# Convolution taps on 32x32 array tiles, four at once, in place of full 128x128 diagonals

## The chip, the cores and the metric

The kernel runs on one core of one Trainium2 chip, in float32 throughout. The metric is device microseconds of one launch; lower is better. Engines are named by what they do: TensorE multiplies matrices (PE in the profile, PEld for its weight loads), VectorE (DVE), ScalarE (ACT) and GpSimd (POOL) do elementwise work, SyncE (SP) issues DMAs.

## The reference

One inference step of a two-layer decoder for 256 prompt rows and 8 sample rows. Each layer is an FFN, a mixer, an FFN. The mixer projects to all its parts at once, and one of them is a depthwise convolution with 31 taps over 256 channels:

```python
def conv_mixer(a, prev, dw, dw_bias, ln_g, ln_b, pw):
    g = a[..., :CONV_W] * jax.nn.sigmoid(a[..., CONV_W:])
    buf = jnp.concatenate([prev.astype(g.dtype), g], axis=1)
    y = lax.conv_general_dilated(buf, dw[:, None, :].astype(g.dtype), window_strides=(1,),
                                 padding='VALID', dimension_numbers=('NWC', 'WIO', 'NWC'),
                                 feature_group_count=CONV_W) + dw_bias
    y = jax.nn.silu(layernorm(y, ln_g, ln_b)) @ pw
    return y, buf[:, -(CONV_K - 1):]
```

Beside it the mixer has a pooling part, sparse attention of the prompt (top 64 of up to 256 keys, chosen by an indexer) and sparse attention of the samples (top 256 of 1025 keys in paged caches of keys and values, 8 pages a sample).

## The kernel before

Channels lie on the 128 partitions and the 264 rows along the free dimension. All weights come as units of 128x1024 (512 KB), 318 in all. SyncE loads a unit into `raw`, ScalarE rounds it into `w_hi` (L338), VectorE makes the remainder `w_lo` (L555), and TensorE multiplies in three passes (L984 to L986), 24 matmuls a unit. Buffers are few (six raw, three split), so each engine is held to the pace of the others. Every engine has its program written out by hand, in order, with semaphore waits; nothing is rescheduled.

In the mixer, TensorE runs 15 projection units. VectorE takes each out of PSUM (`plain`, L642), applies the rotary embedding (`perm` on TensorE, then `rope`), and finds the samples' top 256 by a radix search of eight digits: VectorE counts (`count`, L713), TensorE sums the counts (`digit`, L1078), VectorE reads the digit (L720) and counts again. So TensorE and VectorE hand the search to and fro, one digit a unit, while the projection goes on.

The convolution of the prompt stands between these. For tap k and channel half c, ScalarE makes a 128x128 diagonal of the tap's weights (`taps`, L413, from the identity), into a ring of four pairs, and TensorE multiplies it with the gated input `gp`, shifted by k columns (L1091), and accumulates all 31 taps in PSUM bank 7. The taps are drawn in eleven pieces: 3 after unit 8, 3 after unit 9, 2 behind each of units 10 to 13, 3 after unit 14, 5 beside the keys, 5 and 4 before and after the eighth digit. ScalarE then adds the bias (L462).

After the last tap TensorE computes the prompt's scores (L1200), VectorE masks them (`masked`, L851), ScalarE exponentiates, VectorE divides (`norm`, L862), TensorE transposes (L1231) and multiplies with the values (L1241), and VectorE makes the low part of a head's output (`heads_out`, L886). The samples' keys are multiplied in `keys(b)` (L1188): 0 to 3 before the scores, and 4 to 7 one in each of the four head steps, ahead of that step's output. SyncE fetches the keys and values of samples 4 to 7 (L243): after the weight load that waits for the fourteenth split of the mixer it reads 48 page numbers from the table, loads the first values (L256), then the keys, 32 loads of 64 KB. GpSimd, after unit 14, stores the indexer keys (L1390), fetches 16 value pages (L1394) and stores the pooling state (L1398, L1399, 2048 runs of 60 bytes), then computes the pooling sums.

Of the kernel before, what the change touches and what calls it, by code (L numbers as in the profile page):

```python
# [14 lines left out]
AL = mybir.AluOpType  # L15
# [27 lines left out]
DW = 56  # L43
# [20 lines left out]

PAIRS = 4

# [15 lines left out]
    tanh=2, glu=2, tap=CK, conv=CK, conv_p=1, c_sum=1, c_cent=1, c_sq=1, c_var=1, c_rms=1, c_norm=1, c_silu=1,  # L82
# [9 lines left out]
def build(nc, xT, wts, par, cst, ptab, digits, kT, vC, kxT, scT, spT,  # L92
          yT, okT, ovT, okiT, ocP, ocS, opP, opS):
    ctx = ExitStack()
    with ctx:
# [40 lines left out]
        s_kx = [at[0]]  # L136
        kx = place("kx", [128, 4, PAST], F32)
        kx_end = at[0]
        kv = place("kv", [128, KV, PAST], F32)
# [24 lines left out]
        diag = place("diag", [128, 2 * PAIRS, 128], F32, [s2[0]])  # L164
# [20 lines left out]
        pTs = place("pTs", [128, NPG, 64], F32, s_kx)  # L185
        dg = place("dg", [64, 64], F32)
# [31 lines left out]
        ones = con[:, C_ONE:C_ONE + 128]  # L218

# [113 lines left out]
        def _(act):  # L333
# [67 lines left out]
            def mixer(L):  # L401
                u0 = U_MIX

                taken = [0]

                def taps(upto):

                    for k in range(taken[0], upto):
                        if k >= PAIRS:
                            act.wait_ge(sem["conv"], at_layer(L, "conv", k - PAIRS + 1))  # L410
                        for c in range(2):
                            w = DW + CK * c + k
                            ins = act.activation(diag[:, 2 * (k % PAIRS) + c, :], ident, ACT.Copy,  # L413
                                                 scale=pars[:, w:w + 1])
                        ins.then_inc(sem["tap"], 1)
                    taken[0] = upto

# [24 lines left out]
                taps(4)  # L442
# [5 lines left out]
                taps(8)  # L448
# [9 lines left out]
                taps(CK)  # L458

                act.wait_ge(sem["conv"], at_layer(L, "conv", CK))  # L460
# [86 lines left out]
        def _(dve):  # L547
# [86 lines left out]
            def mixer(L):  # L634
# [92 lines left out]
                dve.wait_ge(tables, 64)  # L727
                dve.wait_ge(sem["rstd"], at_layer(L, "rstd", 1))
# [57 lines left out]
                rope(ak[:, :], 3)  # L786
# [13 lines left out]
                rope(aq[:, 1, :], 3)  # L800
# [10 lines left out]
                for c in range(2):  # L811
# [3 lines left out]
                    if c == 0:  # L815
                        rope(aq[:, 3, :], 3)
# [55 lines left out]
                def equals():  # L872

                    dve.wait_ge(sem["conv"], at_layer(L, "conv", CK))
# [106 lines left out]
        def _(pe):  # L981
# [79 lines left out]
            def mixer(L):  # L1061
# [19 lines left out]
                drawn = [0]  # L1081

                def taps(upto):

                    for k in range(drawn[0], upto):
                        if k == 0:
                            pe.wait_ge(sem["glu"], at_layer(L, "glu", 2))
                            pe.wait_ge(sem["idx_relu"], at_layer(L, "idx_relu", 4))
                        pe.wait_ge(sem["tap"], at_layer(L, "tap", k + 1))
                        for c in range(2):  # L1090
                            ins = pe.matmul(PS[:, 7, NP * c:NP * c + NP], diag[:, 2 * (k % PAIRS) + c, :],  # L1091
                                            gp[:, c, k:k + NP], start=(k == 0 and c == 0), stop=(k == CK - 1),
                                            skip_group_check=True)
                        ins.then_inc(sem["conv"], 1)
                    drawn[0] = upto
# [50 lines left out]
                perm(7, ak[:, :], 3).then_inc(sem["perm"], 1)  # L1146
                taps(3)
                unit(9)

                pe.wait_ge(sem["chunk"], at_layer(L, "chunk", 9))  # L1150
# [4 lines left out]
                taps(6)  # L1155
                pe.wait_ge(sem["v_nat"], at_layer(L, "v_nat", 1))
                digit(0)
                unit(10)
                perm(9, aq[:, 0, :], 2).then_inc(sem["perm"], 1)
                taps(8)  # L1160
                digit(1)
                unit(11)
                pe.wait_ge(sem["rope"], at_layer(L, "rope", 4))
                perm(10, aq[:, 1, :], 3).then_inc(sem["perm"], 1)
                taps(10)
                digit(2)
                unit(12)
                pe.wait_ge(sem["rope"], at_layer(L, "rope", 5))
                perm(11, aq[:, 2, :], 2).then_inc(sem["perm"], 1)
                taps(12)  # L1170
                digit(3)
                unit(13)
                pe.wait_ge(sem["rope"], at_layer(L, "rope", 6))
                perm(12, aq[:, 3, :], 3).then_inc(sem["perm"], 1)
                taps(14)
                digit(4)
                unit(14)
                taps(17)
# [27 lines left out]
                for b in range(KV):  # L1206
                    keys(b)
                    if b == 1:
                        taps(22)
                        digit(6)  # L1210
                taps(27)
                digit(7)
                taps(CK)
# [130 lines left out]
        def _(pool):  # L1344
# [26 lines left out]
            with pool.Fori(0, DEPTH) as L:  # L1371
# [16 lines left out]
                pool.wait_ge(tables, 64)  # L1388
# [157 lines left out]
```

## Time and profile before

| | |
|---|---|
| runs (median; lowest to highest) | 1262.84 us; 1260.96 to 1262.85 us |
| profiled execution | 1260.21 us, span 1258.7 us, mean granted TensorE clock 0.964 |
| TensorE busy | 1162.6 us (92%), 8680 matmul records |
| VectorE busy | 794.2 us (63%) |
| ScalarE busy | 577.0 us (46%) |
| GpSimd busy | 196.0 us (16%) |
| HBM | 153 GB/s over the span |

A float32 matmul leaves two records in the profile, one for each of its passes; the rounded passes L984 to L986 leave one. The granted clock of TensorE is a share of 2.4 GHz and stands at 1.0 or at 0.5. A busy TensorE means only that a record is open, since records of one stream overlap.

### The profile page before, as it was taken

What the parts mean: (1) busy time and instruction counts of PE and PEld (TensorE: products, weight loads), DVE (VectorE), ACT (ScalarE), POOL (GpSimd) and SP (SyncE); (2) the same over time, 40 slices, a digit from 0 to 9 for tenths busy, and PEclk for the clock granted to TensorE, in tenths of its full rate; (3) what the DMA queues carried; (4) which work ended last, traced back from release to release, by engine and by line L of the source; (5) the groups of instructions that cost most, each with busy time, mean ns of one, the idle gap of its engine ahead of it and who ended that gap; (6) DMA issues with size and microseconds to landing.
All of it is one profiled execution on the core that took longest, in us unless ns stands there. A gap on an engine that the chain in (4) does not pass through costs nothing.

```text
span 1258.7 us, 27509 instructions
## 1 busy us (share of the span) xinstructions
PE 1162.6 (92%) x8680; PEld 1085.4 (86%) x8680; DVE 794.2 (63%) x1261; ACT 577.0 (46%) x976; POOL 196.0 (16%) x213
## 2 busy tenths in 40 slices
PE   4999999899779799999889999989996789999996
PEld 4999999778559799999889999977973689999994
DVE  3666644878744766664566665467877357666546
ACT  4444434444344544443454444353544445444435
POOL 0212100201500312110131211020024012121002
PEclk9999999899889899999989999989998899999998
DMA  7455565341643255555436555644418243555551
GB/s 239 164 214 189 178 220 201 111 127 62 116 133 117 69 193 176 183 183 182 135 89 213 183 182 189 226 153 136 101 57 136 85 133 127 184 174 185 182 166 37
DMA packets 91928, 192.92 MB, mean 153 GB/s; under 512 B 11986, under 2 KB 50066, under 8 KB 91730
## 3 DMA queue, kind: packets, MB, share of 16 engines
q1 hardware_dynamic: 89874, 187.58, 45.8%
q0 software_dynamic: 1984, 4.47, 1.6%
q8 instruction: 36, 0.59, 0.2%
q14 instruction: 34, 0.28, 0.1%
HBM read 189.42 MB, written 2.59 MB: 153 GB/s over the span
## 4 chain that ended last, share of the span: by engine, by line
PE 53%; issue 38%; POOL 3%; POOLq 2%; ACT 2%; DVE 1%; DMA 1%; DVEq 0%; SPq 0%; ACTq 0%
PE PS L984 16%; PE PS L985 15%; PE PS L986 15%; PE PS L1010 2%; PE PS L1091 2%; PE PS L1134 1%; POOLq L1393 1%; POOL h L1368 1%; DMA raw<-in_wts 1%; PE PS L1073 1%; ACT w_hi L338 1%; POOL vx L1394 1%; POOLq L1394 0%; DVE w_lo L555 0%; POOL pw L1409 0%
## 5 line engine op out<-in xcount | busy, mean ns | idle before, releaser
L555 DVE TENSOR_TENSOR w_lo<-raw,w_hi 128x1024 fp32r<-128x1024 f32 x312 | 409.4, 1312 | 324.1 <-ACT w_hi L338 321.9
L984 PE MATMUL PS<-x_hi,w_hi 128*128 128x264 f32 x1648 | 487.5, 296 | 10.3 <-DVE w_lo L555 10.3
L985 PE MATMUL PS<-x_lo,w_hi 128*128 128x264 f32 x1648 | 471.9, 286 | 0.0
L986 PE MATMUL PS<-x_hi,w_lo 128*128 128x264 f32 x1648 | 471.6, 286 | 0.0
L338 ACT ACTIVATE w_hi<-raw 128x1024 fp32r<-128x1024 f32 x312 | 328.0, 1054 | 238.0 <-PE PS L986 236.9
L984 PEld LDWEIGHTS PS<-x_hi,w_hi 128*128 128x128 f32 x1648 | 315.6, 192 | 14.5 <-DVE w_lo L555 11.2
L985 PEld LDWEIGHTS PS<-x_lo,w_hi 128*128 128x128 f32 x1648 | 315.8, 192 | 2.5
L986 PEld LDWEIGHTS PS<-x_hi,w_lo 128*128 128x128 f32 x1648 | 313.9, 190 | 0.0
L984 PE MATMUL PS<-h_hi,w_hi 128*128 (+1 forms) x832 | 237.5, 285 | 3.1 <-issue 3.1
L986 PE MATMUL PS<-h_hi,w_lo 128*128 (+1 forms) x832 | 237.1, 285 | 0.0
L985 PE MATMUL PS<-h_lo,w_hi 128*128 (+1 forms) x832 | 236.5, 284 | 0.0
L1357 POOL TENSOR_TENSOR us<-gs,us 128x264 f32<-128x264 f32 x88 | 97.0, 1103 | 437.6 <-DVE us L604 437.6
L984 PEld LDWEIGHTS PS<-h_hi,w_hi 128*128 128x128 f32 x832 | 156.6, 188 | 3.9 <-issue 3.9
L985 PEld LDWEIGHTS PS<-h_lo,w_hi 128*128 128x128 f32 x832 | 157.2, 189 | 0.0
L986 PEld LDWEIGHTS PS<-h_hi,w_lo 128*128 128x128 f32 x832 | 156.9, 189 | 0.0
L377 ACT ACTIVATE gs<-gs 128x264 f32<-128x264 f32 x88 | 37.3, 424 | 198.8 <-DVE gs L598 198.8
L1368 POOL TENSOR_TENSOR h<-h,y 128x264 f32<-128x264 f32 x48 | 44.2, 930 | 434.1 <-DVE y L584 434.1
L1010 PE MATMUL PS<-sq,con 128*128 128x264 f32 x96 | 36.7, 469 | 39.2 <-ACT sq L350 24.0
L1091 PE MATMUL PS<-gp,diag 128*128 128x256 f32 x248 | 57.9, 382 | 0.4 <-ACT diag L413 0.4
L1091 PEld LDWEIGHTS PS<-gp,diag 128*128 128x128 f32 x248 | 46.1, 189 | 10.5 <-ACT diag L413 2.8
L598 DVE TENSOR_TENSOR gs<-PS,rstd 128x264 f32<-128x264 f32 x88 | 38.0, 432 | 25.5 <-PE PS L986 20.1
L1010 PEld LDWEIGHTS PS<-sq,con 128*128 128x128 f32 x96 | 18.3, 233 | 41.2 <-ACT sq L350 26.1
(244 smaller groups left out, 977.2 us busy)
## 6 DMA issues: line engine op xcount, KB each, us to landing
raw<-in_wts SPq DMA_DIRECT2D x315, 512.0 KB, 3.8
kv<-in_kT SPq DMA_DIRECT2D x128, 64.0 KB, 2.5
kx<-in_kxT SPq DMA_DIRECT2D x128, 32.0 KB, 2.1
kv<-in_vC SPq DMA_DIRECT2D x64, 64.0 KB, 1.9
vx<-in_vC POOLq DMA_DIRECT2D x32, 64.0 KB, 2.1
vx<-in_vC SPq DMA_DIRECT2D x32, 64.0 KB, 2.0
h<-in_xT SPq DMA_DIRECT2D x1, 1056.0 KB, 4.9
out_yT<-h SPq DMA_DIRECT2D x8, 132.0 KB, 1.7
```

Source lines behind the costliest of these rows:

```text
L338: act.activation(w_hi[:, u % SPLIT, :], raw[:, u % RAW, :], ACT.Copy).then_inc(sem["w_hi"], 1)
L377: act.activation(gs[:, f % 3, :], gs[:, f % 3, :], ACT.Silu).then_inc(sem["silu"], 1)
L555: tt(w_lo[:, u % SPLIT, :], raw[:, u % RAW, :], w_hi[:, u % SPLIT, :].bitcast(F32), AL.subtract).then_inc(sem["w_lo"], 1)
L598: tt(gs[:, f % 3, :], PS[:, 2 * (f % 3), 0:NT], rstd[:, :], AL.mult).then_inc(sem["gs"], 1)
L984: pe.matmul(out, w_hi[:, w, cols], hi, start=start, stop=False)
L985: pe.matmul(out, w_hi[:, w, cols], lo, start=False, stop=False)
L986: return pe.matmul(out, w_lo[:, w, cols], hi, start=False, stop=stop)
L1010: pe.matmul(PS[:, 7, 0:NT], ones, sq[:, d, :], start=(d == 0), stop=(d == KD - 1)).then_inc(sem["mm_pre"], 1)
L1073: return pe.matmul(PS[:, bank, 0:NT], con[:, which:which + 128], x, start=True, stop=True)
L1091: ins = pe.matmul(PS[:, 7, NP * c:NP * c + NP], diag[:, 2 * (k % PAIRS) + c, :], gp[:, c, k:k + NP], start=(k == 0 and c == 0), stop=(k == ...
L1357: pool.tensor_tensor(us[:, f % 3, :], gs[:, f % 3, :], us[:, f % 3, :], AL.mult).then_inc(sem["mid"], 1)
L1368: pool.tensor_tensor(h[:, d, :], h[:, d, :], y[:, d, :], AL.add).then_inc(sem["h_new"], 1)
```

## The change

The channels are cut into groups of 32, four in each half. A tap of one group is a 32x32 diagonal. It is multiplied on one of the 16 array tiles: the row tile is the channel group i, the column tile j is that of the tap, k = 4r + j. So a round r covers four taps at once. A row tile i accumulates in its own PSUM bank (3, 4, 5, 7), and column tile j writes partitions 32j to 32j + 31 of it, so that after eight rounds each bank holds four partial sums, one over the other. The calls of `taps` are now four, of two rounds each, after units 9 to 12.

ScalarE copies the four banks to `cpart`, and `fold` multiplies them with `stack`, an identity of 32 columns stacked four times, which adds the four partial sums and puts each channel group in its place in bank 7. GpSimd makes all tap tiles `dgw` at once, in two instructions of 128x992, from `stack` and the weights. `dgw` and `cpart` lie where the indexer's cached keys `kx` lay, so GpSimd waits until these are read. VectorE makes `stack` from the identity ahead of the first chunk. The perms use bank 2 alone, and wait for the rope before.

```diff
-                def taps(upto):
-
-                    for k in range(taken[0], upto):
-                        if k >= PAIRS:
-                            act.wait_ge(sem["conv"], at_layer(L, "conv", k - PAIRS + 1))
-                        for c in range(2):
-                            w = DW + CK * c + k
-                            ins = act.activation(diag[:, 2 * (k % PAIRS) + c, :], ident, ACT.Copy,
-                                                 scale=pars[:, w:w + 1])
-                        ins.then_inc(sem["tap"], 1)
...
-                for m, upto in ((12, 10), (13, 12), (14, 14), (15, 17), (16, 17), (17, 19)):
+                for m in range(12, 18):
                     split(L, u0 + m)
-                    taps(upto)
+                    if m == 15:
+                        act.wait_ge(sem["conv"], at_layer(L, "conv", 1))
+                        for i, bank in enumerate(CONV_BANKS):
+                            act.activation(cpart[:, i, :], PS[:, bank, :], ACT.Copy).then_inc(sem["c_part"], 1)
...
-                taps(CK)
-
-                act.wait_ge(sem["conv"], at_layer(L, "conv", CK))
+
+                act.wait_ge(sem["c_fold"], at_layer(L, "c_fold", 1))
...
                 dve.wait_ge(tables, 64)
+                dve.tensor_reduce(stack[:, :], ident.rearrange("p (q c) -> p c q", q=4), AX.X, AL.add) \
+                    .then_inc(sem["stack"], 1)
                 dve.wait_ge(sem["rstd"], at_layer(L, "rstd", 1))
...
                 def equals():
-
-                    dve.wait_ge(sem["conv"], at_layer(L, "conv", CK))
...
+                def taps(first, rounds):
+
+                    for r in range(first, first + rounds):
                         for c in range(2):
...
+                            for j in range(4):
+                                k = 4 * r + j
+                                for i, bank in enumerate(CONV_BANKS):
+                                    if k < CK:
+                                        rows = slice(32 * i, 32 * i + 32)
+                                        ins = pe.matmul(PS[32 * j:32 * j + 32, bank, NP * c:NP * c + NP],
+                                                        dgw[rows, c, k, :], gp[rows, c, k:k + NP],
+                                                        start=(r == 0 and c == 0), stop=(k + 4 >= CK),
+                                                        skip_group_check=True)
...
+                def fold():
+
+                    pe.wait_ge(sem["c_part"], at_layer(L, "c_part", 4))
+                    for i in range(4):
+                        ins = pe.matmul(PS[32 * i:32 * i + 32, 7, :], stack[:, :], cpart[:, i, :],
+                                        start=True, stop=True)
+                    ins.then_inc(sem["c_fold"], 1)
...
+                pe.wait_ge(sem["glu"], at_layer(L, "glu", 2))
+                pe.wait_ge(sem["diag"], at_layer(L, "diag", 2))
+                pe.wait_ge(sem["idx_relu"], at_layer(L, "idx_relu", 4))
...
+                pool.wait_ge(tables, 64)
+                pool.wait_ge(sem["stack"], at_layer(L, "stack", 1))
+                pool.wait_ge(sem["idx_d"], at_layer(L, "idx_d", 1))
+                for c in range(2):
+                    pool.tensor_tensor(dgw[:, c, :, :],
+                                       stack[:, :].unsqueeze(1).to_broadcast([128, CK, 32]),
+                                       pars[:, DW + CK * c:DW + CK * c + CK].unsqueeze(2).to_broadcast([128, CK, 32]),
+                                       AL.mult).then_inc(sem["diag"], 1)
```

TensorE, before, between unit 10 and unit 11 (L1073 is a perm, L1091 a tap of both halves, L1078 a digit):

```order
849 L1073 MATMUL PS<-aq,con 128x264 [waits chunk]
850 L1089 REGISTER_ALU
851 L1091 MATMUL PS<-gp,diag 128x256 [waits tap]
852 L1091 MATMUL PS<-gp,diag 128x256
853 L1089 REGISTER_ALU
854 L1091 MATMUL PS<-gp,diag 128x256 [waits tap]
855 L1091 MATMUL PS<-gp,diag 128x256
856 L1078 MATMUL PS<-rad,con 128x1 [waits count]
```

The same place after the change (L1061 is the perm, L1078 the taps, L1066 the digit):

```order
833 L1061 MATMUL PS<-aq,con 128x264 [waits chunk]
834 L1078 MATMUL PS<-gp,dgw 32x256 x64
835 L1066 MATMUL PS<-rad,con 128x1 [waits count]
836 L977 REGISTER_ALU
```

Four matmuls of the full array have become 64 of one tile each.

TensorE, before, from the seventh digit to the first scores (L1188 are the keys of samples 2 and 3, L1200 and L1201 the scores):

```order
1018 L1078 MATMUL PS<-rad,con 128x1 [waits count]
1019 L1188 MATMUL PS<-kv,LA 64x512 [waits kv_full2]
1020 L1188 MATMUL PS<-kv,LA 64x512
1021 L1188 MATMUL PS<-kv,LA 64x512 [waits kv_full3]
1022 L1188 MATMUL PS<-kv,LA 64x512
1023 L1089 REGISTER_ALU
1024 L1091 MATMUL PS<-gp,diag 128x256 [waits tap]
```

The same stretch after, up to the scores:

```order
958 L1066 MATMUL PS<-rad,con 128x1 [waits count]
959 L1187 MATMUL PS<-kv,LA 64x512 [waits kv_full2]
960 L1187 MATMUL PS<-kv,LA 64x512
961 L1187 MATMUL PS<-kv,LA 64x512 [waits kv_full3]
962 L1187 MATMUL PS<-kv,LA 64x512
963 L1065 REGISTER_ALU
964 L1066 MATMUL PS<-rad,con 128x1 [waits count]
965 L1199 MATMUL PS<-ak,aq 128x256 [waits rope]
```

No tap stands here any more: the eighth digit and the scores follow the keys directly.

## Rows read from the trace of the kernel before

**Rows 1.** Conv taps: group (count, busy us, mean ns), then timeline (start us, us).
```profile
L1091 PE MATMUL PS<-gp,diag 128*128 128x256 f32 x248 | 57.9, 382 | 0.4 <-ACT diag L413 0.4
...
271.54 2.75 PE L1091 MATMUL PS<-gp,diag 128*128 128x256 f32 x12
...
311.04 4.59 PE L1091 MATMUL PS<-gp,diag 128*128 128x256 f32 x20
```

**Rows 2.** Timeline of VectorE, layer 0; idle us before and its releaser in brackets.
```profile
272.57 1.23 DVE L555 TENSOR_TENSOR w_lo<-raw,w_hi 128x1024 fp32r<-128x1024 f32 x1 [2.58 <-ACT w_hi L338]
...
291.24 0.16 DVE L720 TENSOR_SCALAR radi<-PS 128x1 int32<-128x1 f32 x1 [0.45 <-PE PS L1078]
...
293.38 1.23 DVE L555 TENSOR_TENSOR w_lo<-raw,w_hi 128x1024 fp32r<-128x1024 f32 x1
...
301.85 0.16 DVE L720 TENSOR_SCALAR radi<-PS 128x1 int32<-128x1 f32 x1 [1.94 <-PE PS L1078]
...
328.44 0.96 DVE L851 TENSOR_TENSOR sp__106<-PS,bias 128x768 f32<-128x768 f32 x1 [6.61 <-PE PS L1201]
```

**Rows 3.** Timeline of TensorE where it uses part of the array.
```profile
251.03 1.68 PE L1125 MATMUL PS<-ki,qi 64*128 64x256 f32 x16
...
375.21 0.27 PE L1280 MATMUL PS<-kv,pTs 128*8 128x128 f32 x1
375.31 0.27 PE L1280 MATMUL PS<-vx,pTs 128*8 128x128 f32 x1
375.32 0.27 PE L1280 MATMUL PS<-kv,pTs 128*8 128x128 f32 x1
...
262.64 0.39 PE L1138 MATMUL PS<-kn,LQ 128*32 128x1 f32 x8
```

**Rows 4.** Prices of GpSimd and ScalarE: group, timeline, and ScalarE's PSUM copy (ns).
```profile
L1357 POOL TENSOR_TENSOR us<-gs,us 128x264 f32<-128x264 f32 x88 | 97.0, 1103 | 437.6 <-DVE us L604 437.6
...
338.24 2.30 POOL L1408 COPY pw<-pa 64x256 f32<-64x256 f32 x1
...
L440 ACT ACTIVATE X<-PS x1: 1027/1027/1027, 268.2 to 268.2; 128x1024 f32<-128x1024 f32 x1
```

**Rows 5.** Timeline of SyncE's and GpSimd's DMA issues and TensorE, layer 0.
```profile
305.48 0.55 POOL L1390 DMA_DIRECT2D out_okiT<-ki  x1 [27.27 <-PE PS L986]
...
331.48 1.28 POOL L1399 DMA_DIRECT2D out_opS<-stp  x1
...
321.99 5.08 SPq L256 DMA_DIRECT2D vx<-in_vC  x8
327.25 17.16 SPq L243 DMA_DIRECT2D kv<-in_kT  x32
...
339.69 2.49 PE L1188 MATMUL PS<-kv,LA 128*64 128x512 f32 x4
```

**Rows 6.** Tile kv in 330.9 to 331.3, then in 332.5 to 335.5: issue to landing.
```profile
L243 SPq DMA_DIRECT2D kv<-in_kT x1: 345/345/345, 330.9 to 330.9; - x1
...
DMA to landing us min/median/max: 2.1/2.1/2.1
...
L243 SPq DMA_DIRECT2D kv<-in_kT x6: 345/346/346, 332.5 to 335.2; - x6
...
DMA to landing us min/median/max: 7.5/8.3/8.5
```

**Rows 7.** Windows (clock is 0.60), VectorE's first head output twice, layer 1's store and load.
```profile
328.40:339.70 11.30, 4.72 (x23) 3.56 (x23) 10.92 (x19) 4.70 (x18) 9.39 (x12) 0.60 0.93 110
...
347.11 0.42 DVE L886 TENSOR_TENSOR h_lo<-PS,h_hi 128x256 fp32r<-128x256 f32 x1
...
964.93 0.42 DVE L886 TENSOR_TENSOR h_lo<-PS,h_hi 128x256 fp32r<-128x256 f32 x1
...
947.98 1.28 POOL L1399 DMA_DIRECT2D out_opS<-stp  x1
...
L243 SPq DMA_DIRECT2D kv<-in_kT x1: 345/345/345, 948.7 to 948.7; - x1
```

More of the change, by code:

```diff
@@ L81 @@
     o_shi=1, o_slo=1, dg=1,
-    tanh=2, glu=2, tap=CK, conv=CK, conv_p=1, c_sum=1, c_cent=1, c_sq=1, c_var=1, c_rms=1, c_norm=1, c_silu=1,
+    tanh=2, glu=2, stack=1, diag=2, conv=1, c_part=4, c_fold=1, conv_p=1, c_sum=1, c_cent=1, c_sq=1, c_var=1, c_rms=1, c_norm=1, c_silu=1,
     c_hi=1, c_lo=1, c_out=1, c_ohi=1, c_olo=1,
@@ L185, in build @@
         pTs = place("pTs", [128, NPG, 64], F32, s_kx)
+        stack = place("stack", [128, 32], F32)
         dg = place("dg", [64, 64], F32)
@@ L218, in build @@
         ones = con[:, C_ONE:C_ONE + 128]
+        CONV_BANKS = (3, 4, 5, 7)
         def at_layer(L, name, k):
@@ L785, in mixer @@
                 counted_ = count_above_zero()
-                rope(ak[:, :], 3)
+                rope(ak[:, :], 2)
                 signs(counted_)
@@ L799, in mixer @@
                 plain(11, aq[:, 2, :])
-                rope(aq[:, 1, :], 3)
+                rope(aq[:, 1, :], 2)
                 digit(2)
@@ L815, in mixer @@
                     if c == 0:
-                        rope(aq[:, 3, :], 3)
+                        rope(aq[:, 3, :], 2)
                         dve.wait_ge(sem["rope"], at_layer(L, "rope", 8))
@@ L1079, in digit @@
                               start=True, stop=True).then_inc(sem["digit"], 1)
[L1081 to L1089, printed above, removed]
-                        for c in range(2):
-                            ins = pe.matmul(PS[:, 7, NP * c:NP * c + NP], diag[:, 2 * (k % PAIRS) + c, :],
-                                            gp[:, c, k:k + NP], start=(k == 0 and c == 0), stop=(k == CK - 1),
-                                            skip_group_check=True)
-                        ins.then_inc(sem["conv"], 1)
-                    drawn[0] = upto
+                def taps(first, rounds):
+                    for r in range(first, first + rounds):
+                        for c in range(2):
+                            for j in range(4):
[7 more added lines that the diff above has]
+                                                        skip_group_check=True)
+                    if first + rounds == 8:
+                        ins.then_inc(sem["conv"], 1)
+                def fold():
[4 more added lines that the diff above has]
+                    ins.then_inc(sem["c_fold"], 1)
                 first_units(L, 0, u0)
@@ L1145, in mixer @@
                 unit(8)
-                perm(7, ak[:, :], 3).then_inc(sem["perm"], 1)
-                taps(3)
+                perm(7, ak[:, :], 2).then_inc(sem["perm"], 1)
                 unit(9)
+                pe.wait_ge(sem["glu"], at_layer(L, "glu", 2))
+                pe.wait_ge(sem["diag"], at_layer(L, "diag", 2))
+                pe.wait_ge(sem["idx_relu"], at_layer(L, "idx_relu", 4))
                 pe.wait_ge(sem["chunk"], at_layer(L, "chunk", 9))
@@ L1154, in mixer @@
                 ins.then_inc(sem["v_t"], 1)
-                taps(6)
+                taps(0, 2)
                 pe.wait_ge(sem["v_nat"], at_layer(L, "v_nat", 1))
```

34 lines of the change are left out of this document (14 added, 20 removed).

## The prediction

> **What bounds the kernel now.** I read the page first, then TensorE's timeline through the conv taps, VectorE's beside it, and last the queues of SyncE and GpSimd. The page puts TensorE at 92% of the span; the taps are 248 records of 0.382 us [rows 1]. A run of twenty of them stands beside the keys at 311.04. A record is one pass: each float32 matmul leaves two, and 124 records a layer are 31 taps x 2 channel halves x 2 passes. In a run of twelve they start (2.75 - 0.38)/11 = 0.215 us apart [rows 1], so a layer spends 124 x 0.215 = 26.7 us on them. They stand in eleven pieces between projection units, digits of the top-k search and keys.
>
> VectorE's timeline shows who waits. Its idle stretches in layer 0 [rows 2] are 2.58 us for the high half of unit 10, which ScalarE made late because it drew tap diagonals first; 0.25 us, 0.45 and 0.45 before three digits (one stands there); 1.94 us before the fifth digit; 0.23 us at the seventh; and 6.61 us before the first masked scores, at 328.44. With 2.2 us of the first these make 12.1 us in which VectorE waited for TensorE or ScalarE only because the taps stood in line. After 328.44 VectorE is the one that is waited for. The second layer repeats this 617.0 us later.
>
> **What the 16 tiles cost.** The new code issues 248 matmuls of 256 columns a layer, so 496 records, 128 in each of three calls and 112 in the last. If all tiles stream side by side, one tile has 8 records in a call and a call takes 8 x 0.215 = 1.72 us, as much as two taps did; the layer has four calls, 6.9 us. Nothing in the trace runs 16 tiles, so I bound it. For tiles running side by side speak two places [rows 3]: sixteen records on two row tiles (eight each, 4 of 256 and 4 of 128 columns, one stream of which would be 4 x 0.215 + 4 x 0.109 = 1.3 us) take 1.68 us with the last one's latency, where one stream would be 2.6; and two column tiles (names vx and kv) each start a pass every 0.11 us, 0.01 us apart from each other. The second tile starts although the first still has passes queued, so the second pass of each matmul does not hold the next tile. The upper side: on one 32-column tile with one moving column, eight records take 0.39 us [rows 3], and their mean spacing without the last latency (0.17) is about 0.031 us; 128 x 0.031 = 4.0 us a call. The lower side is 1.72. I take 1.72 plus an estimated 0.25 for leaving and entering the full-array form (the two-row-tile block shows 0.1 over its stream).
>
> The Trainium skill, "TensorE: Matmul & The Clock Gate", section "Measured speedup vs the span model", gives 10.6 times for 16 tiles; that is my side. The same page, "Wait — 56ns, not 53.3ns?", says that starts never come closer than about 25 ns, which would speak against it: 3.2 us a call by that figure. The pairs 0.01 us apart in rows 3 contradict it between tiles, not for a long run.
>
> **The change part by part, layer 0, before's clock.**
> (1) Three taps ahead of unit 9 go: it starts at 271.54 instead of 273.94, ends 274.6. The tile waits stand behind it. GpSimd makes the tiles once the sample index scores are done, about 263.2; 2 x 992 elements at 1103 ns per 264 [rows 4] are 8.3 us, done at 271.5, covered by 3 us. The other side is its slowest row, 2.30 us for 256 elements: 17.8 us, done at 281 (a rival below).
> (2) ScalarE loses 62 diagonals x 0.39 = 24 us and copies four banks, each half of the 1.03 us that 1024 columns took [rows 4]: 2.1 us, beside unit 13, needed at the fold 5 us later: nothing. Its freedom moves VectorE's split by 2.2 us.
> (3) First call: 274.9 to 276.85; the digit then waits for the count, 277.2 instead of 280.31: -3.1. Each further stage is unit, perm, call, digit: 5.31 now (291.24 to 301.85 is two of them [rows 2]), 5.56 after. VectorE's own work in a stage is 5.31 - 0.45 = 4.86, so TensorE leads. Digits at 282.9, 288.3, 293.9; the next stage has no call, so the fifth digit is ready at 297.45 instead of 301.5: -4.1.
> (4) The fold is 8 records of 512 columns, 0.9 us on four column tiles, 3.4 on one after the other. It ends by 302, and the keys wait for VectorE's packing (302.9) anyway: nothing either way below 1 us. The 17 taps beside the keys are gone, 14.6 us.
> (5) VectorE now runs from the fifth digit to the masked scores with no stop: 328.44 - 6.61 - 0.23 - 4.1 = 317.5: **-10.9 us**. TensorE, with keys and digits from 302.9 on and the eighth digit waiting for its count at 313.7, gets there at 314.8. The bank that the perms now share adds rope waits; each rope is over 3 us early.
> (6) The new small reduction on VectorE stands ahead of the first chunk of the mixer; 0.16 to 0.43 us by its small and 264-column rows [rows 2]: +0.2.
>
> **What takes part of it back.** The keys of samples 4 to 7 are fetched by SyncE, and keys(4) stands in TensorE's order ahead of the first head's output. SyncE's moment hangs on split 14 (row of 293.38 in [rows 2]): after it come 48 page numbers, eight loads at 321.99, then the 32 key loads [rows 5]. That split follows the digit at 288.3, so it moves only -2.6. GpSimd's chain hangs on unit 14 (305.48 is its first store [rows 5]), moves -4.1, and ends in the store of the pool state at 331.48. Loads issued before it land in 2.1 us; those issued 1 us and more after take 7.5 to 8.5 [rows 6]. Now the eighth load of sample 4 leaves at 330.9, ahead of the store. After: the load at 328.3, the store at 327.4, so it falls into the slow stretch and lands at about 335.1 (3 to 8.5 us after issue: 331.5 to 336.8). Keys(4) was at 339.69 [rows 5] and would be wanted at 328.8: 6.3 us are lost. In layer 1 load and store already leave together (948.7 and 947.98 [rows 7]); after, the load is 2.1 us behind and lands at about 955.2, rel. 338.2: 9.4 us lost. TensorE idles up to there and is at half clock (0.60 granted in 328.4 to 339.7 [rows 7]), so keys(4) takes 3.5 instead of 2.5 us, then output 1.3, copy 0.5. VectorE's first head output (L886) comes at 340.4 instead of 347.11 [rows 7]: **-6.7**; in layer 1 at 343.5 against 347.9 (964.93 less 617.0): **-4.5**. Behind it (norm, two more masks and heads) the order is as before, and the fifth to seventh keys are there by then (the next sample's 12.2 us after the store, as in [rows 6]: 339.6). Nothing later is closer than 8 us to its data.
>
> Sum: -6.7 - 4.5 + 0.4 = **-10.8 us**. The profiled execution spans 1258.7 and took 1260.21 us, so 1249.4; against the median 1262.84 it is **1252.0 us**.
>
> **The rivals.**
> A. The tiles overlap and the collision with the store costs nothing (loads land in 3 us, or the store shifts): -10.9 x 2 + 0.4 = -21.4, 1241.4 us. For it: the slow stretch starts only 1 us after the store, and my gap in layer 0 is 0.9. Against it: layer 1.
> B. Each record costs the 0.031 us of one small tile: a call 4.0 instead of 1.97, unit 14 and the store +8.1, the masked scores only -2.8. The next sample's keys land 12.2 us after the store (issued up to 335.2, 8.5 later [rows 6]), so at 347.7, where they are used at about 345.6 now: 0 to +2 a layer, 1262.8 to 1267. The Trainium skill's 25 ns, the page and section named above, would lie between this and the forecast.
> C. Slower: passes waiting in TensorE's queue stop it from reaching more than four tiles, which is 0.215/4 = 0.054 us a record, 6.9 us a call, +4.9. Four calls: the masked scores +8.8 a layer, +18 in all: 1281. For it: in rows 3 the second column tile begins only when the first has four passes left. It decides from 0.031 us a record up, twice the ideal 0.0134.
> D. GpSimd's tiles come at 281: everything +6.4, masked scores -4.5 a layer, and the keys of sample 4, behind the store, at 341: about 1262.
>
> **How the numbers follow.** Forecast 0.48, A 0.18, B 0.11, C 0.13, D 0.10. The range 1240 to 1268 holds all but C. A measurement of this kernel tells 0.2% (2.5 us) from nothing. Faster: forecast and A, and 0.08 of B and D: 0.74. Same: 0.12. Slower: C and a last hundredth of B: 0.14.
>
> **What would show it.** Tap records start 13 to 15 ns apart and a call lasts 2.0 us; VectorE's masked scores begin near 317.5; TensorE idles before keys(4) to 335; the store of the pool state lies between the key loads. If calls last 4 us or more, step (3) is wrong; if the idle before keys(4) is missing, the last step is.

## The result, and the profile after

The changed kernel takes 1254.74 us (median of five; 1252.51 to 1255.88) against 1262.28 us for the kernel before on the same chip (1260.96 to 1262.85): a ratio of 0.9941, 95% interval 0.9928 to 0.9954. The profiled execution spans 1253.0 us (before 1258.7). I had forecast 1252.0 us, 10.8 us less than the 1262.84 us that stood as the median then; by the medians above 7.5 us were gained, and 5.7 us by the two profiled executions.

The group of the taps, which answers to [rows 1], and that of the keys (busy us, mean ns, idle before):

```profile
L1078 PE MATMUL PS<-gp,dgw 32*32 32x256 f32 x992 | 22.1, 385 | 0.0
...
L1187 PE MATMUL PS<-kv,LA 128*64 128x512 f32 x64 | 35.4, 693 | 13.1 <-DMA kv<-in_kT 11.1
```

The 248 full-array records are gone, and the taps are 992 records of one tile each. New is the last column of the keys: TensorE sat idle 13.1 us before keys, 11.1 of it for a transfer of keys. TensorE's timeline in layer 0 shows the calls (L1078), the digits behind them (L1066), the fold (L1089) and the keys (L1187), then two keys of layer 1:

```profile
275.53 2.76 PE L1078 MATMUL PS<-gp,dgw 32*32 32x256 f32 x128
279.05 0.35 PE L1066 MATMUL PS<-rad,con 128*128 128x1 f32 x2 [0.77 <-DVE rad L702]
...
289.41 2.76 PE L1078 MATMUL PS<-gp,dgw 32*32 32x256 f32 x128
292.10 0.38 PE L1066 MATMUL PS<-rad,con 128*128 128x1 f32 x2
...
305.34 1.07 PE L1089 MATMUL PS<-cpart,stack 128*32 128x512 f32 x8
...
333.04 2.92 PE L1187 MATMUL PS<-kv,LA 128*64 128x512 f32 x4
...
343.92 3.68 PE L1187 MATMUL PS<-kv,LA 128*64 128x512 f32 x4 [5.58 <-DMA kv<-in_kT]
...
949.67 3.51 PE L1187 MATMUL PS<-kv,LA 128*64 128x512 f32 x4 [2.10 <-DMA kv<-in_kT]
...
959.00 3.00 PE L1187 MATMUL PS<-kv,LA 128*64 128x512 f32 x4 [3.44 <-DMA kv<-in_kT]
```

A call of `taps` (two rounds) takes 2.85, 2.69 and 2.55 us from its first record to the digit where the digit follows at once (the last of them has 112 records), not 1.97. The keys of sample 4 start with hardly a wait, those of sample 5 after 5.58 us, and they then take 3.68 us. The same keys before, and the window of TensorE after (the clock is the third number from the end):

```profile
345.61 1.93 PE L1188 MATMUL PS<-kv,LA 128*64 128x512 f32 x4
```

```profile
343.90:349.30 5.40, 5.38 (x16) 2.33 (x17) 1.89 (x4) 0.36 (x2) 0.00 (x0) 0.55 0.70 182
```

TensorE had stood idle for 5.58 us, and most of the stretch behind it ran at 1.2 GHz (0.55 granted), so the late keys cost 1.75 us more than their wait.

VectorE's timeline, the answer to [rows 2] and [rows 7] (L543 is the split, L708 a digit read, L841 the masked scores, L874 the low part of a head's output):

```profile
265.98 2.79 DVE L543 TENSOR_TENSOR w_lo<-raw,w_hi 128x1024 fp32r<-128x1024 f32 x1 [0.23 <-ACT w_hi L340]
...
286.06 0.16 DVE L708 TENSOR_SCALAR radi<-PS 128x1 int32<-128x1 f32 x1 [0.73 <-PE PS L1066]
...
292.52 0.16 DVE L708 TENSOR_SCALAR radi<-PS 128x1 int32<-128x1 f32 x1 [1.61 <-PE PS L1066]
...
298.86 0.16 DVE L708 TENSOR_SCALAR radi<-PS 128x1 int32<-128x1 f32 x1 [1.48 <-PE PS L1066]
...
302.43 0.16 DVE L708 TENSOR_SCALAR radi<-PS 128x1 int32<-128x1 f32 x1 [0.21 <-PE PS L1066]
...
322.33 0.96 DVE L841 TENSOR_TENSOR sp__107<-PS,bias 128x768 f32<-128x768 f32 x1
...
340.05 0.41 DVE L874 TENSOR_TENSOR h_lo<-PS,h_hi 128x256 fp32r<-128x256 f32 x1
...
349.35 0.42 DVE L874 TENSOR_TENSOR h_lo<-PS,h_hi 128x256 fp32r<-128x256 f32 x1 [3.50 <-ACT h_hi L475]
```

The masked scores begin 6.1 us earlier than before (328.44), the first head output 7.1 earlier (347.11 in [rows 7]), and the second only 1.35 earlier (350.70 before): what VectorE had won it lost between two heads. GpSimd makes the tiles, and stores the pooling state at the time it did before ([rows 5], 331.48):

```profile
263.95 3.73 POOL L1385 TENSOR_TENSOR dgw<-stack,pars 128x992 f32<-128x992 f32 x2
...
331.60 1.28 POOL L1403 DMA_DIRECT2D out_opS<-stp  x1
```

The eighth key load of sample 4 left at 331.1 and landed 1.9 us later. The eight of sample 5 were issued from 331.7 to 335.3, right behind the store. The profile has no landing for them; that the last let TensorE go at 343.92 is what it shows.

### The profile page after: what moved, and what is told of

It is laid out like the page before. It is cut to its first block, busy times and chain, and to the rows that moved or that the text cites. A ratio compares the mean times of both kernels' runs of the same rounds, so it can differ in the third digit from the quotient of the medians.

```text
span 1253.0 us, 28803 instructions
## 1 busy us (share of the span) xinstructions
PE 1136.9 (91%) x9440; PEld 1054.1 (84%) x9440; DVE 798.0 (64%) x1263; ACT 541.1 (43%) x860; POOL 202.6 (16%) x217
## 4 chain that ended last, share of the span: by engine, by line
PE 49%; issue 39%; DVE 4%; POOL 3%; ACT 2%; POOLq 2%; DMA 1%; DVEq 0%; SPq 0%; ACTq 0%
PE PS L972 15%; PE PS L973 15%; PE PS L974 15%; PE PS L998 2%; PE PS L1078 1%; DVE w_lo L543 1%; POOLq L1397 1%; POOL h L1364 1%; DMA raw<-in_wts 1%; ACT w_hi L340 1%; DVE wk L665 1%; PE PS L1061 1%; POOL vx L1398 1%; DVE wk L676 0%; POOLq L1398 0%
## 5 line engine op out<-in xcount | busy, mean ns | idle before, releaser
L543 DVE TENSOR_TENSOR w_lo<-raw,w_hi 128x1024 fp32r<-128x1024 f32 x312 | 412.8, 1323 | 319.1 <-ACT w_hi L340 317.0
L1187 PE MATMUL PS<-kv,LA 128*64 128x512 f32 x64 | 35.4, 693 | 13.1 <-DMA kv<-in_kT 11.1
L572 DVE SCALAR_TENSOR_TENSOR y<-y,pars,rstd_post 128x264 f32<-128x264 f32 x48 | 39.9, 852 | 0.2
```

The costliest lines, as they stand in the source:

```text
L543: tt(w_lo[:, u % SPLIT, :], raw[:, u % RAW, :], w_hi[:, u % SPLIT, :].bitcast(F32), AL.subtract).then_inc(sem["w_lo"], 1)
L572: stt(y[:, d, :], y[:, d, :], pars[:, gain + d:gain + d + 1], rstd_post[:, :], AL.mult, AL.mult).then_inc(sem["y_new"], 1)
L1187: ins = pe.matmul(PS[0:64, 4 + c, :], LA[:, b, :], kv[:, b % KV, 512 * c:512 * c + 512], start=(b == 0), stop=(b == NB - 1))
```

## The experiments

**Does the store hold the keys back?** Four kernels move it or what it meets. The first moves it in the changed kernel, the second does the same to the kernel before.

```
-                with pool.Fori(0, NPG) as g:
+                with pool.Fori(0, 2) as g:
...
+                pool.wait_ge(sem["pool_c"], at_layer(L, "pool_c", 1))
+                pool.dma_start(opP[bass.ds(L, 1)].rearrange("a p c k -> p (a c) k"), pp[:, :, NP:]).then_inc(stored, 16)
+                pool.dma_start(out4(opS), stp[:, :, :, 1:]).then_inc(stored, 16)
+                with pool.Fori(2, NPG) as g:
...
-                pool.dma_start(opP[bass.ds(L, 1)].rearrange("a p c k -> p (a c) k"), pp[:, :, NP:]).then_inc(stored, 16)
-                pool.dma_start(out4(opS), stp[:, :, :, 1:]).then_inc(stored, 16)
```

> The changed kernel, but GpSimd stores the pooling state (out_opP, out_opS) after the first 4 of its 16 value pages instead of after the last, so about 313 us instead of 331.6, where no keys or weights are fetched. Theory 1 (the keys of sample 5 come 5.6 us late in layer 0 and those of sample 4 and 5 come 2.1 and 3.4 us late in layer 1 because the store of 2048 short runs holds the DMA engines): the idle of TensorE before keys(5) goes from 5.58 us to under 1 us, loads issued in 331 to 335 land in 2 to 3 us, the sample scores start 3 to 4 us earlier in each layer, and the launch takes about 1247 us (1245 to 1250). Theory 2 (the loads are late because SyncE and GpSimd between them issue too many bytes; the store only happens to stand there): the idle stays over 3 us and the time stays within 2 us of 1254.7.

Measured: 1246.85 us, ratio 0.9888 (0.9874 to 0.9902), so 7.9 us below the changed kernel (6.9 us if each is taken from the kernel before as measured beside it). The timelines of GpSimd and TensorE, then the eight loads of sample 5 (tile kv in 331.2 to 335.2) and the value pages behind the moved store (tile vx in 314 to 322):

```profile
312.77 1.28 POOL L1403 DMA_DIRECT2D out_opS<-stp  x1
...
333.20 3.68 PE L1187 MATMUL PS<-kv,LA 128*64 128x512 f32 x4 [1.16 <-DMA kv<-in_kT]
...
339.43 1.93 PE L1187 MATMUL PS<-kv,LA 128*64 128x512 f32 x4
...
L245 SPq DMA_DIRECT2D kv<-in_kT x8: 345/346/346, 331.4 to 335.0; - x8
...
DMA to landing us min/median/max: 1.7/1.9/2.0
...
L1407 POOL DMA_DIRECT2D vx<-in_vC x6: 534/534/556, 314.3 to 321.7; - x6
...
DMA to landing us min/median/max: 2.0/5.0/8.2
```

The same loads at the same time now land in 1.9 us, and the 5.58 us are gone. The delay went with the store: the value pages behind it land in up to 8.2 us, and have the time. Theory 1 stands. Both stores of the pooling state moved together here (`opP` as well as the 2048 runs of `opS`), so these runs don't say what each of the two costs.

> The kernel before, with the same move of the two stores and nothing else. There keys(5) starts at 345.61, one piece behind its last load (343.70), and VectorE, not the keys, sets the first head output. Theory 1 (before, VectorE sets the pace up to the third head, so the late keys cost it at most 1 to 2 us a layer): 1259 to 1262 us, at most 3 us below the kernel before. Rival (the store costs both kernels alike, so the change itself is worth 7.5 us with either placing): about 1255 us.

Measured: 1262.15 us, ratio 1.0004 (0.9995 to 1.0013). Theory 1 again (0.15 us above its range): the stores cost the kernel before nothing that can be measured. So the two changes aren't additive: the taps alone give 7.5 us, the stores alone nothing, both together 14.5.

The third puts the stores behind the pooling sums.

> The changed kernel, with the two stores of the pooling state behind the pooling sums, so at about 341 us instead of 331.6, when all but the last keys are fetched and the values of the samples begin. Theory (what the store costs is what it collides with, and the keys of sample 5 are the only load without slack): TensorE's idle before keys(5) goes, the values have 10 us of slack and are late by less, 1246 to 1250 us. Rival (the store always costs about what it did, only elsewhere; the values or the first weights of the output are late by 8 us): 1253 us or more.

Measured: 1251.63 us, ratio 0.9930 (0.9916 to 0.9943), between the two, and neither number was right. The timeline of TensorE's keys in layer 1, GpSimd's store, and the last two loads of sample 7:

```profile
950.01 1.93 PE L1187 MATMUL PS<-kv,LA 128*64 128x512 f32 x4
...
963.13 3.04 PE L1187 MATMUL PS<-kv,LA 128*64 128x512 f32 x4 [2.04 <-DMA kv<-in_kT]
...
954.90 1.24 POOL L1415 DMA_DIRECT2D out_opS<-stp  x1
...
L245 SPq DMA_DIRECT2D kv<-in_kT x2: 345/346/346, 955.4 to 955.9; - x2
...
DMA to landing us min/median/max: 4.0/5.5/7.1
```

Sample 5 is on time, in layer 0 TensorE's keys no longer wait at all, and 3 us are gained there. In layer 1 the store falls on the last two loads of sample 7, which land in up to 7.1 us, and the layer keeps nothing of what it was ahead. What the stores cost hangs on what is issued behind them.

The fourth asks what bounds the kernel once the keys are in time: SyncE reads its page numbers eight at a time behind the last six weight loads.

```
+                places, order = {}, (0, *range(KV, NB), 1)
                 for n in range(n, end):
                     unit(n)
-                places = {b: [page(g + b * NPG) for g in range(NPG)] for b in (*range(KV, NB), 0, 1)}
+                    if n >= end - 6:
+                        b = order[n - (end - 6)]
+                        places[b] = [page(g + b * NPG) for g in range(NPG)]
```

> The kernel with the early store (1246.85 us), and SyncE reads its 48 page numbers eight at a time behind each of the six last weight loads, where it waits for splits anyway, instead of all behind the last. The first values and keys of samples 4 to 7 are then issued from about 305 us (unit 14) instead of 322.9. Theory (in e1 TensorE waits 1.2 us for the last load of keys(4), issued only 2 us before, in layer 0 and 1 to 3 us in layer 1, and it then runs the keys at half clock): the wait goes, keys(4) starts with the stream, and the launch gains 2 to 5 us: 1242 to 1245 us. Rival (VectorE's norms and masks set the first two head outputs either way, as its row without idle up to 339 shows): within 1 us of 1246.85.

Measured: 1249.14 us, ratio 0.9901 (0.9886 to 0.9916): nothing gained, rather 2.3 us lost. SyncE's first values and keys, then TensorE's keys(4) and VectorE's first head output:

```profile
306.51 5.09 SPq L258 DMA_DIRECT2D vx<-in_vC  x8
311.78 19.07 SPq L245 DMA_DIRECT2D kv<-in_kT  x32
...
333.77 3.21 PE L1190 MATMUL PS<-kv,LA 128*64 128x512 f32 x4
...
340.59 0.41 DVE L877 TENSOR_TENSOR h_lo<-PS,h_hi 128x256 fp32r<-128x256 f32 x1
```

The keys come 15 us earlier and TensorE doesn't wait for them, yet the first head output comes no earlier after the masked scores (17.4 us, as in e1). VectorE sets it, so the 1.16 us in e1 were covered: the rival holds. Most of the loss is no effect of the edit. Of 2.5 us between the two profiled executions, 1.8 are there when VectorE makes the split beside GpSimd's tiles (266.89 instead of 265.08), before SyncE can read the first page early (behind its load at 269.76), and 1.2 of these come at 30 to 40 us. The windows of e1, then of e9 (the clock is the third number from the end):

```profile
30.00:40.00 10.00, 8.06 (x66) 8.06 (x67) 6.46 (x10) 5.65 (x9) 3.33 (x2) 1.00 0.51 160
```

```profile
30.00:40.00 10.00, 8.42 (x57) 8.43 (x58) 6.71 (x9) 4.26 (x7) 2.41 (x2) 0.83 0.50 161
```

The granted clock is 0.83 where it was 1.00, so part of the stretch ran at 1.2 GHz. Why in the one and not in the other these runs don't show.

**What sets the pace of 16 tiles?** A set is the 16 matmuls of one round and half, 32 records. In the changed kernel a set starts every 0.65 us, where two passes of 256 columns take 0.43. One kernel halves the columns, one halves the tiles, one changes the order of the tiles. Each was run once, for the length of its calls, and the first two leave out part of the taps.

```
+                        w = NP if r == 0 else NP // 2
...
-                                        ins = pe.matmul(PS[32 * j:32 * j + 32, bank, NP * c:NP * c + NP],
-                                                        dgw[rows, c, k, :], gp[rows, c, k:k + NP],
+                                        ins = pe.matmul(PS[32 * j:32 * j + 32, bank, NP * c:NP * c + w],
+                                                        dgw[rows, c, k, :], gp[rows, c, k:k + w],
```

> The changed kernel, but the taps of rounds 1 to 7 multiply only 128 of the 256 columns of each half, so the other 128 lack those taps. 128 records a call as before. Theory 1 (the pace of the 16 tiles is set by handing out records, about 0.0167 us each with a step of 0.13 us in every 32): the three later calls stay at 2.6 to 2.9 us. Rival (the tiles are busy streaming 256 columns, several waiting for each other): the three later calls fall to 1.3 to 1.6 us.

```
-                                    if k < CK:
+                                    if k < CK and (r == 0 or i < 2):
```

> The changed kernel, but rounds 1 to 7 multiply only row tiles 0 and 1, so channels 64 to 127 of each half lack those taps; a set is 8 tiles of 256 columns instead of 16, a later call 64 records. Of the 0.64 us of a set of 16, 0.43 are two passes of 0.215 us. Theory (the other 0.21 us is handing out, 0.013 us for each of the 16 matmuls, and isn't covered by the stream): a set of 8 takes 0.54 us, the three later calls 2.1 to 2.3 us. Rival 1 (a fixed cost of 0.21 us whenever the set comes round to the same tile): unchanged, 2.6 to 2.9 us. Rival 2 (all of it is covered once half the records are gone): 1.7 to 1.9 us.

The third call of TensorE's timeline in each, the half columns first:

```profile
289.46 1.90 PE L1079 MATMUL PS<-gp,dgw 32*32 32x128 f32 x128
```

```profile
289.75 1.96 PE L1078 MATMUL PS<-gp,dgw 32*32 32x256 f32 x64
```

Both fall to 1.9 us, where I had expected 2.6 to 2.9 and 2.1 to 2.3; the rival of the half columns, 1.3 to 1.6, missed too. By handing out I mean what it takes to start one record after another. Eight tiles of 256 columns keep exactly the pace of the stream (sets start 0.431 us apart, two passes of 0.215): all handing out is covered, rival 2. Sixteen tiles of half the columns take 0.43 us a set as well, although their stream needs only 0.21: there something that goes with the number of matmuls sets the pace, at 0.027 us each. I call it handing out, but each matmul also brings the load of its 32x32 weights (0.10 us long in the profile), and no run here parts the two. With 16 tiles and all columns, stream and handing out would each need 0.43 us, and a set takes 0.65. So the tiles do stream side by side, and something between the two doesn't overlap once both are full; what, these runs don't tell.

```
-                            for j in range(4):
-                                k = 4 * r + j
-                                for i, bank in enumerate(CONV_BANKS):
+                            for i, bank in enumerate(CONV_BANKS):
+                                for j in range(4):
+                                    k = 4 * r + j
```

> The changed kernel with the 16 matmuls of a round and half in the other order: all four taps of one row tile in a row, instead of all four row tiles of one tap. Theory (a set of 16 costs its stream of 0.43 us and another 0.21 us for handing out, whatever tile comes next): calls stay at 2.6 to 2.9 us. Rival (neighbours on one row tile get in each other's way, or those on one column tile do now): the calls change by over 0.4 us.

The second call of layer 0:

```profile
284.18 2.92 PE L1078 MATMUL PS<-gp,dgw 32*32 32x256 f32 x128
```

Measured: records of 2.76, 2.92, 2.76 and 2.62 us in the four calls, to the hundredth those of the changed kernel. The order doesn't matter.

**What do the calls cost on the path?** With the early store, first six of the eight rounds are left out.

> The kernel with the early store and only rounds 0 (ahead of the first digit) and 7 (ahead of the fourth): 8 of 31 taps, 23 are left out. This prices what the tap calls still cost on the path. Theory (VectorE sets the pace to the masked scores and its 0.73 + 1.61 + 1.48 us of idle is the taps' whole price): 3.0 to 4.0 us less a layer, 1239 to 1241 us. Rival (sample keys, issued at SyncE's own pace, are the next bound at once): over 1244 us.

Measured: 1240.32 us, 6.5 us below e1: 3.3 us a layer, as the theory said. That is less than half of what TensorE was spared: its calls shrank by about 8 us a layer. VectorE no longer waits before any of the first five digits, so it sets the pace, and unit 14 ends 4.1 us earlier (GpSimd's store behind it leaves at 301.04, in e1 at 305.16). The rival is there as well, behind it: TensorE waits again for the keys of sample 4.

```profile
331.29 3.60 PE L1185 MATMUL PS<-kv,LA 128*64 128x512 f32 x4 [2.72 <-DMA kv<-in_kT]
```

So 3.3 us is what the calls beyond two rounds cost with that wait counted in, not the whole price of the taps. Next, the same rounds placed otherwise: 3, 1, 1, 1, 1 ahead of five digits, and 1 behind the fifth.

> The kernel with the early store (1246.85 us), and the eight rounds of taps placed 3, 1, 1, 1, 1 ahead of the first five digits and the last one behind the fifth digit, instead of 2, 2, 2, 2 ahead of the first four. TensorE has 0.77 us of idle before the first digit, and VectorE idles 0.73, 1.61, 1.48 and 0.21 us before the next four because a stage with two rounds takes TensorE 6.4 us against 5.3 us of VectorE's. Theory (with the keys no longer late, VectorE sets the pace up to the masked scores, so what it waits for the taps is all paid): its four gaps shrink to 0.2 to 0.5 us each, the masked scores start 2.5 to 3 us earlier in each layer, and the launch takes 1241 us (1240 to 1243.5). Rival (the keys of samples 4 and 5 are issued at SyncE's own pace and come too late again, TensorE waiting 3 to 4 us before keys(4)): 1245 to 1247 us.

Measured: 1246.54 us (1244.88 to 1248.98), no different from e1. Neither side was right: the keys weren't late (0.52 us in layer 0, 0.81 in layer 1). VectorE's gaps before the second to the fourth digit shrank to 0.25 to 0.34 us, as I said, but one of 0.38 us came before the first, and that before the fifth became the largest. The fourth and fifth digit of VectorE's timeline, then TensorE's first call:

```profile
297.53 0.16 DVE L708 TENSOR_SCALAR radi<-PS 128x1 int32<-128x1 f32 x1 [0.33 <-PE PS L1066]
302.72 0.16 DVE L708 TENSOR_SCALAR radi<-PS 128x1 int32<-128x1 f32 x1 [1.83 <-PE PS L1066]
...
276.61 3.32 PE L1078 MATMUL PS<-gp,dgw 32*32 32x256 f32 x153
280.32 1.28 PE L1078 MATMUL PS<-gp,dgw 32*32 32x256 f32 x39 [0.38 <-issue]
```

From the first call to the fifth digit TensorE stops for 0.8 us in e1 and 0.4 in e5. I had read VectorE's idle as slack to be won by placing the taps better; it is TensorE's work that has to be done there, wherever it stands. Counted from the first call, the masked scores came 0.8 us earlier in layer 0 and 0.4 in layer 1, too little to show in the launch. And the call of three rounds has a stop that the calls of two in e1 don't have: after 153 of its 192 records TensorE stands for 0.38 us in layer 0 and 1.14 us in layer 1 without a wait that the profile shows. Why, no run here tells.

**Does GpSimd hold VectorE off?** VectorE's split at 265.98 took 2.79 us instead of 1.23, ending 1.1 us behind GpSimd's tiles (267.68). One kernel makes the tiles in 16 instructions.

```
+                    for k in range(0, CK, 4):
+                        m = min(4, CK - k)
+                        w = DW + CK * c + k
+                        ins = pool.tensor_tensor(dgw[:, c, k:k + m, :],
+                                                 stack[:, :].unsqueeze(1).to_broadcast([128, m, 32]),
+                                                 pars[:, w:w + m].unsqueeze(2).to_broadcast([128, m, 32]),
+                                                 AL.mult)
+                    ins.then_inc(sem["diag"], 1)
```

> The changed kernel, but GpSimd makes the tap tiles in 16 instructions of 4 taps (3 in the last of each half) instead of 2 of 31. Theory 1 (VectorE's split at 265.98 took 2.79 us instead of 1.23 because it could not start before GpSimd's instruction had ended at 267.68, one instruction holding the other off): the split takes 1.3 to 1.7 us, the first digit stands 0.7 to 0.8 us earlier, the idle of 0.77 us on TensorE before it goes; the launch gains 0 to 1.5 us, since the keys of sample 5 wait for the store all the same. Rival (the two share the memory ports by turns throughout): the split still takes over 2.3 us, and the tiles take as long or longer.

Measured: 1254.56 us, ratio 0.9952 (0.9938 to 0.9966), no gain, as expected while the keys wait. The split and the tiles in layer 0, then in layer 1:

```profile
266.22 1.28 DVE L543 TENSOR_TENSOR w_lo<-raw,w_hi 128x1024 fp32r<-128x1024 f32 x1 [0.23 <-ACT w_hi L340]
...
264.19 7.15 POOL L1388 TENSOR_TENSOR dgw<-stack,pars 128x128 f32<-128x128 f32 x16
...
877.57 4.88 DVE L543 TENSOR_TENSOR w_lo<-raw,w_hi 128x1024 fp32r<-128x1024 f32 x1 [0.23 <-ACT w_hi L340]
...
875.99 6.68 POOL L1388 TENSOR_TENSOR dgw<-stack,pars 128x128 f32<-128x128 f32 x16
```

In layer 0 theory 1 holds: VectorE gets through, the first digit comes 0.6 us earlier (0.8 counted from the first call: TensorE's idle of 0.77 us is gone), and GpSimd takes twice as long. In layer 1 it falls: each of GpSimd's instructions is 0.42 us, and VectorE stood for 3.65 us, some nine of them, longer than behind the two large ones (2.05 us, the split taking 3.28). The Trainium skill, "SBUF — State Buffer", section "Who interferes with whom", says that a VectorE instruction with two inputs in SBUF contends for a shared port with a GpSimd instruction that reads SBUF, and that the second one to issue is fully blocked until the first finishes. By that rule pieces should help in both layers; layer 0 agrees, the 4.88 us of layer 1 don't.

> The kernel of e5_spread with the tap tiles in 16 GpSimd instructions, as in e4. The first count is then ready 1.2 us earlier, but three rounds of taps end only at about 279.5 and VectorE has other work until 280.4, so Theory 1: within 1 us of e5_spread, 0 to 1.5 us a layer if VectorE's whole line moves up by the 1.3 us that the split no longer loses (1239 to 1242 us). Rival (TensorE now leads in the first stage): no difference within 0.5 us.

Measured: 1249.22 us (1243.21 to 1251.78), ratio 0.9895 (0.9873 to 0.9916): the runs of this one kernel lie 8.6 us apart, wider than the question, so unclear.

> The kernel of e9_pages_early with the tap tiles in 16 GpSimd instructions as in e4. Theory (with no keys to wait for, what VectorE's split lost to GpSimd is paid in full): TensorE's idle of 0.77 us before the first digit goes, digits come 0.6 us earlier in each layer, and the launch gains 1.0 to 1.5 us over e9. Rival (as in e4 and e6 nothing comes of it, another wait takes it up): within 0.5 us of e9.

Measured: 1251.07 us, ratio 0.9925 (0.9912 to 0.9939), 1.9 us more than e9. Neither: layer 1's split takes 4.92 us here too, so what layer 0 wins layer 1 loses. That explains no gain; why it is 1.9 us more stays open.

The best kernel is e1, one pair of stores moved, 14.5 us (1.1%) below the kernel before; e5 can't be told from it.

## Why the prediction was right, and where not

The time is right to 2.7 us, and the forecast's mechanism held in outline: the taps off the path, VectorE first to gain, and a part given back to a collision of key loads with the store. Of the 10.8 us forecast 7.5 came, and some terms missed by more than the sum. Its terms, for layer 0 (start of unit 9, calls, fold and store by their own engine, the others by VectorE's timeline):

| step | forecast | measured |
|---|---|---|
| start of unit 9 | 271.54 | 272.11: 0.5 of the 0.57 is there from the first 27 us of the launch, before any edit |
| (6) stack reduction | +0.2 a layer | 0.30 us long, +0.23 |
| (1) tap tiles | 8.3 us, covered | 3.73 us, but they held VectorE's split back by 1.56 us; first digit at 279.05, not 277.2 |
| (3) call | 1.97 us | 2.85, 2.69, 2.55 us |
| (3) stage | 5.56 us | 6.6, 6.5, 6.3 us |
| (3) fifth digit | -4.1 us | +0.6 us |
| (2), (4) copies, fold | hidden; 0.9 us | 2.06 us, hidden; 1.07 us on four column tiles |
| (5) masked scores | 317.5 (-10.9) | 322.33 (-6.1) |
| store of the pooling state | 327.4 | 331.60 |
| first head output | 340.4 (-6.7) | 340.05 (-7.1) |
| second head output | as the first | 349.35 (-1.35) |
| first head output, layer 1 | 343.5 (-4.5) | 954.35, so 337.35 (-10.6, 2.0 of it brought along from layer 0) |
| end of the mixer | -6.7, layer 1 -4.5 | -2.0, layer 1 -3.4 |

**The mis-sized term is the call.** I added 0.25 us once to a stream of 1.72, which takes 16 tiles for 16 times the speed of one. The call costs 0.2 us more in each set behind the first: about 2.7 us, and three stages of 0.8 to 1.0 us more (0.6 to 0.9 in the call, 0.2 around it). It lies between the forecast and rival B (4.0). The prediction counts the 10.6 times of the Trainium skill, "TensorE: Matmul & The Clock Gate", section "Measured speedup vs the span model", for its side. Here 16 x 0.43 us one after the other against the measured 0.65 is 10.6 times as well, where its own sum had taken 16; whether the two figures count the same thing isn't shown.

The masked scores missed by 4.8 us. Of these 0.57 are the late start; 0.45 the first call; 0.83 the held split, which is what e4 takes away in layer 0; 2.7 the three stages; 0.1 the next, and 0.15 lie between the fifth digit and the masked scores.

**A cost I had put at nothing.** Step (1) asked only when GpSimd's tiles are ready, not whom GpSimd stops meanwhile. They were ready early; the work beside them wasn't free (0.83 us of the first digit in layer 0, by e4).

**The last step hit the wrong sample.** The mechanism is shown (e1, e2), but with unit 14 at its old place the store didn't move, sample 4 went ahead of it, and sample 5 behind. My own rule, the next sample's keys 12.2 us after the store, gives 331.6 + 12.2 = 343.8; they started at 343.92. In the prediction I had used it at 327.4 and found 339.6, in time. So "the order behind it is as before" is the sentence that failed in layer 0, and it failed through the call. In layer 1 both samples were hit (2.10 and 3.44 us). The first head output of layer 0 was met to 0.4 us by luck, two misses against each other: 4.8 us less won up to the masked scores, and in their place keys of sample 4 that weren't late. Then the second head lost 5.7 us against the first, which the forecast hadn't: sample 5's keys, 5.58 us late and 1.75 us longer at half clock, less what slack there was. So layer 0 gave 2.0 us for 6.7, and layer 1 gave 3.4 for 4.5.

**Rivals.** A (the collision costs nothing) is refuted for this kernel and is what e1 brings about: 1246.85 us, not 1241.4, for the most part because of the longer calls and the held split. B (0.031 us a record) is refuted by 0.020, though the number of records does count, as it said. C (four tiles at once, 0.054 us a record) is refuted by 0.020, and by e12: eight tiles stream together. D (tiles at 281) by 267.68.

## What to carry over

When work leaves the path, follow every engine's next transfer and ask which it now meets: here a pair of stores, one of 2048 short runs, cost nothing before, 7 to 8 us after, and nothing that shows once moved by 19 us. Price small-tile matmuls by handing out as well as by streaming (here 0.027 us a float32 matmul, 0.040 with both full), and price an instruction on GpSimd also by what VectorE can't do meanwhile. Idle time of an engine is only to be won if the one that it waits for has a gap in the same stretch.

## What the runs showed of the hardware

- Behind the pair of stores of 60-byte runs (1.28 us to issue the larger), loads land late whichever engine issues them: keys by SyncE (up to 8.5 us, [rows 6]) and value pages by GpSimd (in e1 8.2 us, then 7.0, 5.5, 4.4 and 3.1, and 2.0 for the one issued 8.9 us behind the store). The last of them is there 8.1 us (e11) to 12.3 us (layer 0 of the changed kernel, by what then started) after the store is issued. A load issued 0.5 us ahead of it landed in 1.9 us.
- Tiles of 32x32, 256 columns in float32: 8 at once keep the full rate of the stream (0.431 us a set), 16 bring 1.33 times that (0.65), not twice.
- GpSimd's tile instructions (1.9 us for 992 elements a partition) stopped a VectorE subtraction of 1.23 us for 1.56 us in layer 0 and 2.05 us in layer 1, while VectorE's top-8 searches beside them kept their times. VectorE's norm is longer too where it stands beside the pooling sums, in the changed kernel; that these hold it off is read from their times alone, no run moves them:

```profile
340.58 3.16 DVE L852 TENSOR_TENSOR sp__107<-sp__107,sps 128x512 f32<-128x512 f32 x2
...
340.46 1.29 POOL L1413 TENSOR_TENSOR pw<-pw,con 128x528 f32<-128x528 f32 x1
341.83 1.62 POOL L1415 TENSOR_TENSOR pw<-pw,xp 128x528 f32<-128x528 f32 x1
```

  The same norm takes 1.03 us at 328.73. It stands between the first two head outputs, on VectorE's path in e1, so the next thing to try is to place the sums elsewhere; that wasn't done.
- Executions of one kernel differ by 2 to 4 us (e1: 1246.25 to 1248.6, e5: 1244.88 to 1248.98), in e6 by 8.6, and profiles show stretches at 1.2 GHz that come and go between them, at 30 to 40 us for one (granted 1.00 in e1, 0.83 in e5 and e9). A change of 1 us a layer can't be told from that here.
